# Splitting plain weight slots in operations of 1024 columns, two neighbouring parts each, instead of 512

## What is computed

```python
for l in range(DEPTH):                        # 2 layers
    h = rms_norm(x, attn_pre_g[l])
    u = h @ w_in[l]                           # 1024 x 2560
    y = concat(conv(u), retention(u), moba(u), pool(u))
    x = x + rms_norm(y @ w_out[l], attn_post_g[l])          # 1024 x 1024
    h = rms_norm(x, ffn_pre_g[l])
    f = silu(h @ w_gate[l]) * (h @ w_up[l])   # 1024 x 2816, twice
    x = x + rms_norm(f @ w_down[l], ffn_post_g[l])          # 2816 x 1024
```

## Time and profile before

| | |
|---|---|
| time, median of 3 runs | 1042.85 us (1042.81, 1042.85, 1044.27) |
| the profiled execution | 1043.23 us, of which 1041.4 us are the span of the profile |
| PE busy | 1022.5 us, 98% of the span |
| DVE busy | 892.8 us, 86% |
| ACT busy | 545.9 us, 52% |
| TensorE clock granted | 0.999 of full speed |
| plain splits | 202 operations of 512 columns on DVE, as many on ACT from `raw`; 134 of 1024 columns on each |

### The profile page before, as it was taken

One profiled execution on the slowest core, in us unless ns is written; L12 is line 12 of the kernel. 1 busy time (PEld: TensorE's weight loads), 2 busy tenths in 40 slices (PEclk: granted clock), 3 DMA queues, 4 the chain that ended last, 5 costly groups with the idle time before them and its releaser, 6 DMA issues.

```text
span 1041.4 us, 21345 instructions
## 1 busy us (share of the span) xinstructions
PE 1022.5 (98%) x8474; PEld 833.7 (80%) x8474; DVE 892.8 (86%) x1787; ACT 545.9 (52%) x978; POOL 65.2 (6%) x86
## 2 busy tenths in 40 slices
PE   7999999999999999999999999999999999999997
PEld 5888895597888888888588888846878888888873
DVE  6999988986789999887889888988858989998766
ACT  5635455653657666435554463455546666654241
POOL 1000000020111220000000000001002112100000
PEclk9999999999999999999999999999999999999999
DMA  9622402183487883435413231224437787734222
GB/s 340 188 80 68 137 25 99 52 202 72 118 220 172 217 205 113 165 100 168 156 61 132 72 113 51 82 82 118 96 84 200 189 218 173 191 121 145 80 64 81
DMA packets 72883, 136.69 MB, mean 131 GB/s; under 512 B 8656, under 2 KB 8912, under 8 KB 72656
## 3 DMA queue, kind: packets, MB, share of 16 engines
q1 hardware_dynamic: 62992, 117.50, 34.5%
q0 software_dynamic: 9792, 17.83, 11.3%
HBM read 133.20 MB, written 2.10 MB: 130 GB/s over the span
## 4 chain that ended last, share of the span: by engine, by line
PE 87%; DVE 7%; DMA 3%; ACT 2%; issue 1%; SPq 1%; ACTq 0%; DVEq 0%
PE ps L698 32%; PE ps L806 30%; PE ps L875 14%; PE ps L902 4%; PE ps L702 3%; DMA raw<-weights_dram 2%; DVE ring L1713 2%; PE ps L1033 1%; DVE E L1877 1%; PE ps L1017 1%; DVE E L1829 1%; DMA xs<-x_dram 1%; PE ps L952 1%; SPq L634 0%; PE ps L937 0%
## 5 line engine op out<-in xcount | busy, mean ns | idle before, releaser
L1713 DVE SCALAR_TENSOR_TENSOR ring<-raw,ring 128x512 f16<-128x512 f32 (+2 forms) x368 | 320.5, 902 | 57.9 <-ACT ring L1103 57.6
L1103 ACT ACTIVATE ring<-raw 128x512 f16<-128x512 f32 (+2 forms) x368 | 279.1, 796 | 116.6 <-DVE raw L1678 58.5
L698 PE MATMUL ps<-hT,ring 128*128 128x256 f16 (+1 forms) x1632 | 195.3, 279 | 0.0
L698 PEld LDWEIGHTS ps<-hT,ring 128*128 128x128 f16 x1632 | 159.4, 98 | 28.8
L806 PE MATMUL ps<-hT,ring 128*128 128x256 f16 x1224 | 145.4, 273 | 0.0
L806 PE MATMUL ps<-E,ring 128*128 128x256 f16 x1224 | 144.7, 273 | 0.0
L698 PE MATMUL ps<-ring,hT 128*128 128x256 f16 x1152 | 133.3, 273 | 1.3 <-DVE hT L1837 1.2
L806 PEld LDWEIGHTS ps<-E,ring 128*128 128x128 f16 x1224 | 119.8, 98 | 13.8
L806 PEld LDWEIGHTS ps<-hT,ring 128*128 128x128 f16 x1224 | 119.8, 98 | 13.9
L698 PEld LDWEIGHTS ps<-ring,hT 128*128 128x128 f16 x1152 | 112.1, 98 | 16.3 <-issue 1.9
L1877 DVE SCALAR_TENSOR_TENSOR E<-E,par 128x256 f32<-128x256 f32 x240 | 102.0, 477 | 0.2
(11 more groups left out here) (175 smaller groups left out, 1149.6 us busy)
## 6 DMA issues: line engine op xcount, KB each, us to landing
raw<-weights_dram SPq DMA_DIRECT2D x402, 256.0 KB, 3.6
raw<-weights_dram POOLq DMA_DIRECT2D x68, 256.0 KB, 5.3
gbc<-gains_dram SPq DMA_DIRECT2D x8, 512.0 KB, 5.5
xs<-x_dram SPq DMA_DIRECT2D x4, 512.0 KB, 7.1
U<-weights_dram SPq DMA_DIRECT2D x8, 256.0 KB, 8.0
out_dram<-xs SPq DMA_DIRECT2D x8, 256.0 KB, 2.0
cst<-consts_dram SPq DMA_DIRECT2D x1, 1296.0 KB, 12.5
bd<-pool_w_dram SPq DMA_DIRECT2D x8, 16.0 KB, 9.6
```

Source lines behind the costliest of these rows:

```text
L698: ins = mm(dst, st, mv_, start=first and i == 0, stop=last and i == 2, **kw)
L1103: return A(dst, src, ACT.Copy, scale=scale)
L1713: V.scalar_tensor_tensor(out=at[1], in0=src, scalar=W_SCALE, in1=at[0], op0=ALU.mult, op1=ALU.subtract).then_inc(lo_split, 1)
```

## The change

Two neighbouring parts of a plain slot (0 and 1, or 2 and 3), from slot 3 of layer 0 on, are split by one operation of 1024 columns on ACT and one on DVE, where their two homes in `ring` lie in a row. ACT waits for both parts to land; each operation raises its semaphore by two.

```diff
+        def both(n, part):
+            at = AT_QUAD[n]
+            plain = n >= 3 and n % SLOTS < DN0 and not fast(n)
+            return plain and at[part // 2 * 2 + 1] == at[part // 2 * 2] + 1
...
+                elif both(n, part):
+                    if part % 2 == 0:
+                        for e in range(2):
+                            _, landed, value = raw_home(i + e)
+                            act.wait_ge(landed, value)
+                        copy(quads2(n, part, 0), raw_pair(i), W_SCALE).then_inc(hi_split, 2)
...
                 n = PARTS * slot + part
+                if both(slot, part):
+                    if part % 2 == 0:
+                        dve.wait_ge(hi_split, n + 2)
+                        V.scalar_tensor_tensor(out=quads2(slot, part, 1), in0=raw_pair(n), scalar=W_SCALE,
+                                               in1=quads2(slot, part, 0), op0=ALU.mult,
+                                               op1=ALU.subtract).then_inc(lo_split, 2)
+                    return
```

## The result

The changed kernel takes 1046.32 us, median of 7 runs (1045.75 to 1047.04), beside 1042.85 us for the kernel before (7 runs, 1042.36 to 1044.27): a ratio of 1.003 with a 95% interval of 1.0021 to 1.0040, so 3.5 us slower. The forecast was 1044.7 us with a range up to 1045.9. The direction came out as forecast; the size is 1.6 us larger, and lies outside the range. The profiled execution took 1046.02 us, 2.8 us more than that of before.

What follows compares the result with a forecast made beforehand. The prediction took PE, busy 98% of the span, as the bound, with time moving only through its stalls. Terms +0.38, +0.11, +1.14, -0.21 and +0.41 sum to +1.83 us on 1042.85: 1044.7 us, range 1043.3 to 1045.9.

Steps and rivals of the forecast that it cites:

- The change of layers, +1.14: Splits of slots 1 and 2 of layer 1 delay `q_sums` by 0.78 us and `y_sum` by 1.14 us; PE's stall becomes 1.43 us.
- The mixers of layer 0, +0.11: `ret_state` stands behind the split of slot 11, which DVE would finish at 107.01 in place of 106.90: +0.11 us.
- Layer 1's attention product, -0.21: Four pairs ahead free DVE 0.25 us sooner, so PE's whole 0.21 us stall at layer 1's first attention product goes.
- The start, +0.38: Slot 3's last pair delays the norm behind it on DVE; PE's 0.53 us stall at 38 us grows by 0.38 us.
- Before the feed-forward part, +0.41: In layer 1, joined splits of slot 17 let part 1 of slot 19 load one issue later: +0.41 us on PE's stall.
- DVE as the limit (1): Rival: DVE is the real limit, cheaper splits remove 2.9 us of stalls after the start, giving 1040.0 us; chance 0.04.
- That all stays under cover (2): Rival: each pair's second part has landed when the first begins, so only +0.5 us, 1043.3 us; chance 0.22.
- The transfers before slot 19 (3): Rival: before layer 1's feed-forward part they lose more than one issue, sum +3.0 us, 1045.9 us; chance 0.14.

## Why the prediction was wrong

The step that failed is the sum, by way of its premise that the change can move the time "only through PE's stalls": it took the output at the end for fixed. It lacks a term of +1.16 us for the last store (3.18 in place of 2.02 us). In sixteen profiles the five with 2112 instructions on DVE all have it, the eleven with 2113 all lack it, with joined pairs or without; in timed runs it is 1.33 us. With it the forecast's sum is 1.83 + 1.16 = 2.99 us, 1045.8 us; the 0.5 us that are left to 1046.3 lie within the interval of the measurement (2.2 to 4.2 us over before).

The chains to PE's stalls were the right ones, and PE ended 1.60 us later for a forecast 1.83. That this is so near is in part luck, since terms too large and too small nearly cancel:

- **The change of layers, +1.14.** Right in mechanism, a little small: the stall grew by 1.36 us. The halves alone give 0.55 and 0.43 us. The excess is within what landings differ by (0.29 to 1.36 us of stall in kernels with the old order and no pair joined in slots 0 to 2 of layer 1).
- **The mixers of layer 0, +0.11.** The stall is 0.55 us in each of the three profiles in which slot 11 is joined and 0.34 or 0.35 in the others: +0.20, between the forecast and its upper bound.
- **Layer 1's attention product, -0.21.** Right: the stall is gone where the pairs ahead of it are joined, and stands at 0.21 us in every profile where they are not.
- **The start, +0.38.** The stall shrank to 0.35 us where 0.91 was forecast, because PE came to it later in this execution; the pass behind it started 0.23 us later. By time the pairs of slot 3 alone, at the old program length, cost 0.3 us by the medians and nothing by the ratio, with an interval of about 0.9 us either way. Not resolved.
- **Before the feed-forward part, +0.41.** Not borne out: the stall grew by 0.16 us. The delay of the loads is there. The first line is of the kernel before, the others of the changed kernel:

```profile
717.58 0.43 SPq L624 DMA_DIRECT2D raw<-weights_dram  x1
...
717.34 2.35 DVE L1706 SCALAR_TENSOR_TENSOR ring<-raw,ring 128x1024 f16<-128x1024 f32 x2
...
718.58 0.80 SPq L625 DMA_DIRECT2D raw<-weights_dram  x2
...
719.43 0.43 SPq L630 DMA_DIRECT2D raw<-weights_dram  x1
...
724.22 0.86 POOL L684 DMA_DIRECT2D raw<-weights_dram  x1 [1.01 <-DMA raw<-weights_dram]
...
731.40 2.00 ACT L1109 ACTIVATE ring<-raw 128x1024 f16<-128x1024 f32 x2 [5.21 <-DMA raw<-weights_dram]
```

  The extra load (L630, before L624) goes out 2.09 us after the split of slot 17 began, not 1.68 (it began at 715.90), so 0.41 us later as forecast. But it took 4.79 us to POOL's second sum in place of 5.21, so that this sum stands 6.88 us behind the split, as before (6.89). The stall is 1.11 us, and 0.30 and 0.31 us in two other kernels with slot 17 joined; with it single 0.45 to 1.97 us. The transfers' own times differ by more than the delay.

The rivals: DVE as the limit (1) is refuted, since 52 cheaper splits away from the chains left the time where it was. That all stays under cover (2) fails at the change of layers. The transfers before slot 19 (3) did not lose more; the time lay near that rival's for another reason. The rule weighed in the prediction held: the Trainium skill, "Perfetto Trace Analysis", section "Optimizing Scalar/DVE Operations", says that breaking up instructions may let work finish sooner where an engine that is not saturated makes others idle, and the trace agrees (the pairs of slot 2 alone lengthen PE's stall from 0.29 to 0.72 us).

## What to carry to other kernels

Join splits where the engine behind has slack, and leave them fine where a chain to the bounding engine's next stall runs through them: all 61 pairs cost 3.5 us, of which some 1.2 us go with the length of the program, and the 52 away from the chains cost nothing that can be measured. Nothing is clearly won either: the best version, which also puts `y_sum` where DVE would wait for ACT, measured below before twice, clear of noise once. A sum over stalls must also go through the tail, where nothing covers a transfer. And before a difference of a microsecond is explained by the work that was changed, run a kernel that has the old work and the new program length.

## What the runs showed of the hardware

Program text is fetched while the kernel runs, in packets of 8 KB (0.3 us for the one in the last store) and, 67 times, of 16 KB. In all five profiles with 2112 instructions on DVE an 8 KB fetch starts as the last store's data end, and the last of the store's 16 signals is 1.16 us late. The fetch keeps to DVE's program: in these five it comes 1.86 us after DVE's last operation, in the eleven profiles with 2113 instructions 8.4 us before that operation ends. Why one instruction makes this difference is not settled; only these two lengths were run.

The 16 KB packets seem to do the same to loads (about 1 us each). At the change of layers one falls near slot 1's last load in every profile (in the changed kernel at 496.13, for 0.97 us). In four profiles, three of them of kernels with no pair near, the load's last signal came 0.8 to 1.5 us behind the one before it, and PE's stall was 0.81 to 1.62 us in place of 0.29. Over all sixteen profiles the last signal of a weight load that SP issues came more than 0.5 us behind the fifteenth in 516 of the 1092 loads (47%) with a 16 KB fetch in the 1.5 us before the fifteenth, and in 622 of the other 5340 (12%). So late signals go with fetches, but a fetch neither always brings one nor is needed for one. That the fetch is the cause stays argued, since no run moved it.
